# Strassen's seven products for the up-projections of two MLP blocks, weights stationary, 128 tokens moving

## The reference, cut to what matters

```
def sqrelu_mlp(h, w1, w2):
    a = jax.nn.relu(h @ w1)
    return (a * a) @ w2

for layer in range(DEPTH_2):                  # DEPTH_2 = 2
    ...
    h = h + mixer(rmsnorm(h, mix_norm[layer]))
    h = h + sqrelu_mlp(rmsnorm(h, mlp_norm[layer]), mlp_w1[layer], mlp_w2[layer])
```

## Time and profile before

| | |
|---|---|
| median of 3 runs (lowest, highest) | 1879.67 us (1878.62, 1880.48) |
| span of the profiled execution, from its first to its last instruction | 1877.3 us |
| what lies around that span, against the median | 2.4 us |
| PE, PEld, DVE, ACT busy | 97%, 53%, 27%, 19% |
| granted TensorE clock | 0.996 of full speed over the span |

### The profile page before, as it was taken

The page is one execution under the profiler, slowest core; times in us unless marked ns, Lnnn a source line. Parts: engine busy times, 40 slices in busy tenths (PEclk is TensorE's granted clock), DMA queues, the critical chain, the costliest instruction groups (busy, mean ns, idle before and its releaser), DMA issues. The chain is left out here.

```text
span 1877.3 us, 21793 instructions
## 1 busy us (share of the span) xinstructions
PE 1824.7 (97%) x8661; PEld 998.6 (53%) x8662; DVE 505.1 (27%) x1093; ACT 348.3 (19%) x688; POOL 10.9 (1%) x14
## 2 busy tenths in 40 slices
PE   6999899999999999999999999999999999999998
PEld 5757533333333333333333336768885466788743
DVE  1754411111011111011111104542025443211355
ACT  3221411111111111111111113332000032220001
POOL 0000000000000000000000000000000000000001
PEclk9999899999999999999999999999999999999999
DMA  9986599999999999999999999423355443134252
GB/s 401 324 184 276 207 416 430 431 432 432 431 431 431 433 431 431 431 431 432 431 431 430 432 429 328 155 105 105 135 176 177 146 174 135 45 135 158 86 170 102
DMA packets 101218, 558.43 MB, mean 297 GB/s; under 512 B 16936, under 2 KB 33805, under 8 KB 74413
## 3 DMA queue, kind: packets, MB, share of 16 engines
q1 hardware_dynamic: 98612, 553.06, 72.4%
q10 hardware_dynamic: 2554, 4.63, 1.9%
HBM read 552.43 MB, written 5.23 MB: 297 GB/s over the span
## 5 line engine op out<-in xcount | busy, mean ns | idle before, releaser
L1362 PE MATMUL ps<-ring,xs 128*64 128x512 f32 x2112 | 466.9, 593 | 8.5 <-DMA ring<-in_w_up 4.7
L1362 PEld LDWEIGHTS ps<-ring,xs 128*64 128x64 f32 x2112 | 151.1, 137 | 312.7 <-issue 293.9
L1416 PE MATMUL ps<-ring,actT 128*64 128x512 f32 x1056 | 233.9, 595 | 0.0
L2149 PE MATMUL ps<-hT,ring 128*128 128x256 f32 x1024 | 222.0, 379 | 0.2 <-ACT hT L1614 0.2
L2149 PEld LDWEIGHTS ps<-hT,ring 128*128 128x128 f32 x1024 | 194.3, 190 | 27.0 <-ACT hT L1614 0.6
L2174 PE MATMUL ps<-ring 128*128 128x512 f32 x448 | 192.8, 592 | 0.0
L1416 PEld LDWEIGHTS ps<-ring,actT 128*64 128x64 f32 x1056 | 73.1, 137 | 158.5 <-issue 131.7
L1489 DVE TENSOR_SCALAR hT<-ps 128x512 f32<-128x512 f32 x33 | 22.8, 692 | 448.0 <-PE ps L1362 448.0
L2174 PEld LDWEIGHTS ps<-ring 128*128 128x128 f32 x448 | 85.0, 190 | 105.8 <-issue 105.7
L1937 PE MATMUL ps<-hT,ring 128*128 128x256 f32 x512 | 117.9, 383 | 4.3 <-ACT hT L1614 2.9
L1937 PEld LDWEIGHTS ps<-hT,ring 128*128 128x128 f32 x512 | 94.7, 190 | 23.2 <-issue 5.9
(11 more groups left out here) (434 smaller groups left out, 1548.1 us busy)
## 6 DMA issues: line engine op xcount, KB each, us to landing
ring<-in_w_up SPq DMA_DIRECT2D x64, 2048.0 KB, 23.2
ring<-in_w_down SPq DMA_DIRECT2D x64, 2048.0 KB, 24.2
ring<-in_w_gate SPq DMA_DIRECT2D x64, 2048.0 KB, 22.7
ring<-in_mlp_w SPq DMA_DIRECT2D x16, 2048.0 KB, 7.7
ring<-in_mlp_w SPq DMA_DIRECT2D x32, 1024.0 KB, 5.3
ring<-in_w_mod SPq DMA_DIRECT2D x8, 2048.0 KB, 15.4
ring<-in_odd_w_in SPq DMA_DIRECT2D x6, 2048.0 KB, 7.7
ring<-in_w_mod SPq DMA_DIRECT2D x8, 1024.0 KB, 14.1
```

The costliest lines, as they stand in the source:

```text
L1362: mm = pe.matmul(ps[SLOTS * half:SLOTS * (half + 1), bank, :], xs[:, c % 4, c // 4 * SLOTS:(c // 4 + 1) * SLOTS], weights(v, 8 * part + c) ...
L1416: mm = pe.matmul(ps[SLOTS * half:SLOTS * (half + 1), Y, :], actT[:, f % 4, f // 4 * SLOTS:(f // 4 + 1) * SLOTS], weights(v, 16 + f)[:, hal ...
L2149: mm = pe.matmul(ps[:, bank + f // 2, (f % 2) * SEQ:(f % 2 + 1) * SEQ], mlp_w1[layer][g % 2][:, c, f * P:(f + 1) * P], hT[:, c, :], start= ...
```

## The change

Both up-projections are done by Strassen's algorithm in Winograd's form. The 1024 channels are cut in two halves, the 256 tokens in two halves of 128, and the 512 columns of a group in two halves of 256. Tokens give quarters A11, A12, A21, A22, weights B11 to B22. Seven products of a 128-token quarter (or a sum of such) with a 512x256 quarter of weights (or a sum of such) take the place of eight. A product is 4 chunks by 2 blocks of 128 columns, that is 8 matmuls with 128 tokens moving.

What is new on the other engines:

- DVE, `up_weights`: four sums of weights per group, each 128x1024. `up_tokens`: four sums of tokens per layer, 128x512. `up_sums`: seven additions per group, 128x256 each, which read the products in PSUM and write the hidden values to SBUF.
- ACT, `first_of_group`: product 1 is copied to SBUF; `activate`: relu and square of a group, both in SBUF. The square leaves DVE.
- SP: `w1` has three buffers in place of two, so three groups are loaded ahead, and the first four pairs of `w2` come after, at the end of the up-projection, in place of before it.
- A group takes four banks of PSUM (7 products of 256 columns in 4 x 512), two groups take all eight.
- The variance columns move behind group 1; the rows of `w2` are paired in another order, so that pair c needs groups up to c // 2 alone.

```diff
-    mlp_w1 = [[ring_cols(0), ring_cols(12)], [ring_cols(8), ring_cols(4)]]
+    mlp_w1 = [[ring_cols(a) for a in at] for at in ((0, 12, 8), (8, 4, 0))]
...
-    UP = ((2, 4), (6, 0))
+    UP = (((2, 3, 4, 5), (6, 7, 0, 1)), ((6, 7, 0, 1), (2, 3, 4, 5)))
+    UP_AT = {1: (0, 0), 6: (0, SEQ), 2: (1, 0), 7: (1, SEQ), 5: (2, 0), 4: (2, SEQ), 3: (3, 0)}
...
@@ SP
+            group(0, 2)
...
-            for g in range(2, GROUPS):
-                sp.wait_ge(up_ps, g - 1)
+            for g in range(3, GROUPS):
+                sp.wait_ge(up_ps, 4 * (g - 2))
                 group(0, g)
-            sp.wait_ge(up_ps, GROUPS - 1)
+            sp.wait_ge(up_ps, 4 * (GROUPS - 2))
+            couple(0, 0)
+            couple(0, 1)
+            sp.wait_ge(up_ps, 4 * (GROUPS - 1))
+            couple(0, 2)
+            couple(0, 3)
...
@@ PE
-                        mm = pe.matmul(ps[:, bank + f // 2, (f % 2) * SEQ:(f % 2 + 1) * SEQ], mlp_w1[layer][g % 2][:, c, f * P:(f + 1) * P],
-                                       hT[:, c, :], start=(c == 0), stop=(c == C - 1))
+                token, weight = {1: (A11, B11), 2: (A12, B21), 3: (up_s[3], B22), 4: (A22, T[:, 3]), 5: (up_s[0], T[:, 0]),
+                                 6: (up_s[1], T[:, 1]), 7: (up_s[2], T[:, 2])}[n]
+                for k in range(4):
+                    if ready is not None:
+                        ready(k)
+                    for i in range(2):
+                        mm = pe.matmul(out[:, i, :], weight[:, k, i * P:(i + 1) * P], token[:, k, :],
+                                       start=(opens and k == 0 and i == 0), stop=(k == 3), skip_group_check=True)
...
+                for g in range(1, GROUPS):
+                    pe.wait_ge(w1_in[g % 3], 16 * (W1_TURNS[g % 3] * layer + g // 3 + 1))
+                    pe.wait_ge(up_t_ok, 4 * (GROUPS * layer + g + 1))
+                    if g >= 2:
+                        pe.wait_ge(up_sum, 7 * (GROUPS * layer + g - 1))
...
@@ ACT
-                    act.activation(hid4[...], ps[:, bank:bank + 2, :]..., ACT.Relu).then_inc(relu_ok, 1)
+                    first_of_group(layer, g)
+                    activate(layer, g)
@@ DVE
+                v.tensor_tensor(T[:, 0], B12, B11, ALU.subtract).then_inc(up_t_ok, 1)
+                v.tensor_tensor(T[:, 2], B22, B12, ALU.subtract).then_inc(up_t_ok, 1)
+                v.tensor_tensor(T[:, 1], B22, T[:, 0], ALU.subtract).then_inc(up_t_ok, 1)
+                v.tensor_tensor(T[:, 3], B21, T[:, 1], ALU.subtract).then_inc(up_t_ok, 1)
...
+            def expand(layer, turn):
+                up_tokens(layer, turn)
+                for g in range(1, GROUPS):
+                    up_weights(layer, g)
+                    up_sums(layer, g - 1)
+                    if g == 2:
+                        inverse_variance(layer, UP[layer][1][3], SEQ)
                 split(layer, 0)
+                up_sums(layer, GROUPS - 1)
+                for c in range(1, PAIRS):
                     split(layer, c)
```

## The result

| | before | after |
|---|---|---|
| median | 1879.14 us (1878.60 to 1880.48, 4 runs) | 1858.61 us (1858.05 to 1860.45, 4 runs) |
| span of the profiled execution | 1877.3 us | 1856.2 us, time 1858.05 |
| TensorE's clock over the span | 0.996 | 0.996 |

The ratio is 0.9893, with a 95% interval of 0.9881 to 0.9905. The forecast was 1858.8 us, in a range of 1855 to 1868.

A forecast was written before the change was run, and what follows sets the result against it. TensorE alone was taken to set the time, its matmuls covering 97% of the span. A gain of 21.1 us less 0.2 gave 20.9; 1877.3 - 20.9 = 1856.4, with 2.4 around the span 1858.8 us, range 1855 to 1868.

The forecast's parts named there:

- A pass of 128 columns costs its load, 111.7 ns: Up-projections on TensorE: each pass of 128 moving columns takes as long as its weight load, read from short stretches, 111.7 ns.
- 21.1 us over both layers by passes: Up-projections: 896 passes at 0.1117 us, 100.1 us per layer against 110.6 before, a gain of 21.1 us over both.
- The variance columns lose 0.2: Their 8 passes have no load taken ahead any more: 0.9 us against 0.79, 0.2 us lost in both layers.
- The entry: Start of each MLP: DVE's token and weight sums end before TensorE needs them, thinnest cover 2.3 us, cost nothing.
- The steady groups: Later groups of the up-projections: DVE's 7.9 us per group hides under TensorE's 12.5, weight sums ready 7 us ahead.
- The transfers: Loads of w1: a group lands 7.7 us after issue, and with three buffers DVE wants it 12.5 us after.
- Waits at nothing: TensorE's semaphore waits at group borders and in groups 0 were taken to cost nothing; 6.2 us if each showed.
- Rival (b): Up-projections: waits at borders show, so the gain is smaller by up to 6.2 us, time 1865; chance 0.16.
- The hand-over: Start of the down-projection: DVE splits pair 1 while TensorE works 6 us on pair 0; cover 2 us, cost nothing.
- Rival (c): Hand-over to the down-projection or entry late by sums or weights: 2 to 3 us in a layer, 1863; chance 0.06.
- Rival (a): All 1792 up-projection passes: loads are exposed in the long stream and the kernel is slower, 1945 at 160 ns; chance 0.08.
- The bound of 160 ns: Upper bound for a 128-column pass, taken from four passes at L1336; it would mean a loss of 65 us.

## Why the prediction was right, point by point

- **A pass of 128 columns costs its load, 111.7 ns** (the value taken against bounds of 108 and 160): measured 111.8 in the long pieces of both layers. The products with fewer tokens (32 columns no faster) show that it is not the columns, and the narrower load (109 ns between loads of 64 columns) that it is the load.
- **21.1 us over both layers by passes**: 21.0 in the chain, entry and variance columns included. Per layer, 14.3 us won by seven products for eight, 3.8 lost by halving the moving operand.
- **The variance columns lose 0.2**: their piece has the old 0.79 us, where 0.9 was expected. A small term, over-sized.
- **The entry**: the sums of tokens were expected from 1305.4, the weight sums of group 1 to end at 1313.8, TensorE at group 1 at 1316.1. The timeline of the changed kernel has them as follows:

```profile
1305.35 0.69 DVE L2606 TENSOR_TENSOR spare<-hT 128x512 f32<-128x512 f32 x1 [0.37 <-ACT hT L1614]
...
1312.14 1.23 DVE L2600 TENSOR_TENSOR ring<-ring 128x1024 f32<-128x1024 f32 x1
...
1315.99 1.95 PE L2188 MATMUL ps<-hT,ring 128*128 128x128 f32 x16
```

  The cover was 2.6 us; three more sums, which need 3.7, used it up and left 1.13.
- **The steady groups**: DVE was counted at 7.9 us per group by mean durations; it is busy 7.2 of 12.5, since its instructions overlap. The last weight sum for the group that starts at 1354.5 ends at 1347.2, 7.3 us ahead, where 7 was expected:

```profile
1345.96 1.23 DVE L2600 TENSOR_TENSOR ring<-ring 128x1024 f32<-128x1024 f32 x1
```

  The step that carries the result is the order, and the turned order shows its price.
- **The transfers**: a group of w1 lands 8.3 us (median) after its issue in the changed kernel, not 7.7. Three buffers cover that; issued one group later, as above, it shows.
- **Waits at nothing**: shown with 1728 of them, and the piece of 75.15 us has the borders of six groups inside without a pause. Rival (b) falls.
- **The hand-over**: DVE splits pair 1 from 1404.97, and TensorE needs it 6 us after 1404.59. The rows of the changed kernel (first and last sum of the pair):

```profile
1404.97 0.68 DVE L2798 TENSOR_TENSOR ring<-ring 128x512 f32<-128x512 f32 x1
...
1407.98 0.28 DVE L2807 TENSOR_TENSOR ring<-ring 128x128 f32<-128x128 f32 x1
```

  It is ready at 1408.3, 2.3 us ahead. In the second layer, where the weights of pair 2 come late, DVE waits 1.45 us for them and has the pair split at 1760.7, 3.6 us before TensorE has done pairs 0 and 1 (28 passes from 1752.22). Rival (c) falls.
- **Rival (a)**, the loads slipping in a long stream, falls: in streams of 672 and 960 float32 passes the distance is 111.8 ns, 1.035 times 108. The bound of 160 ns was a misreading. The four passes of L1336 follow a stream whose loads have 64 columns (L1362), and their starts are 223, 122 and 120 ns apart: the first is like the distance behind a change of width in the run with the shorter load (213 ns there), and an average with it is no pace of a stream. The Trainium skill, page "TensorE: Matmul & The Clock Gate", section "Back-to-back issue gap", has about 81 ns per matmul in a stream at 128 columns where an isolated one has about 56, and the prediction carried this ratio of 1.45 over. The traces do not agree with it for these float32 passes: 1.035.

No sizeable error was there to be cancelled: the passes of a layer were put at 100.1 us and take 100.16 in the first, the other terms are within 0.2 us, and the down-projections are unchanged.

## What to carry to other kernels

Cutting the moving operand to save columns pays only down to the length of a weight load; find that length in a short stretch where matmuls move few columns, and multiply by the number of loads, not of columns. When a new algorithm gives work to another engine, its busy share says little: count when each result is ready against when it is asked for, and put what the next group needs ahead of what only the present one needs. A cover can be measured by adding work until it shows. And where a part that no edit touches varies by more than the effect, compare the lengths of the stage and not the totals.

## What was not expected of the hardware

- Pauses of TensorE of 5.2 to 7.7 us were followed by passes at 1.2 GHz, and a group of 12.5 us then took 14.2 to 15.2 (with the pauses filled: 12.7 to 12.8), about 2 us per pause. In the run with six more sums, pauses of 4.9 and 4.2 us did the same (15.56 and 14.37), and pauses of 1.8 us left the group at 12.74 us.
- A change between 64 and 128 loaded columns cost about 0.15 us each time (10.5 us over 72 changes), and made a kernel with less to load slower.
- Waits on satisfied semaphores, two per matmul of two passes, cost nothing even where loads stand end to end.
